# Per-head products with 64-row contraction: zero-padded 128-row operands replaced by row tiles in pairs of PSUM banks

## The reference, cut to what matters

```python
# attention scores of a head, 256 queries by the keys, 64 features summed
z = jnp.einsum('bhqd,bhkd->bhqk', qb, kb) * scale          # stick-breaking attention, 8 heads
# the same kind of product stands in the sparse attention (4 heads, two branches,
# and 15 compressed keys), in the retention (4 heads), and in the chunked RWKV
# recurrence, where for chunks c of 128 tokens and 4 heads
#   M_ab = b^T a, M_ak = k^T a, M_rb = b^T r, M_rk = k^T r   (128 x 128 each, 64 features summed)
```

## Time and profile before

| what | before |
|---|---|
| time, median of 3 (lowest, highest) | 2041.87 us (2037.39, 2044.82) |
| span of the profiled execution | 2041.5 us |
| PE busy, share of the span | 1951.0 us, 96% |
| PE weight loads | 1747.7 us, 86% |
| DVE busy | 1423.1 us, 70% |
| ACT busy | 1168.1 us, 57% |
| POOL busy | 76.5 us, 4% |
| mean granted TensorE clock | 0.990 |

### The profile page before, as it was taken

How to read it: one execution, slowest core, us unless ns; L and a number is a source line. 1 busy time by engine, 2 the same in 40 slices (tenths; PEclk the granted TensorE clock), 3 DMA queues, 4 the chain that set the end, 5 groups by cost and what they waited for, 6 DMA issues and landing times.

```text
span 2041.5 us, 29505 instructions
## 1 busy us (share of the span) xinstructions
PE 1951.0 (96%) x12546; PEld 1747.7 (86%) x12546; DVE 1423.1 (70%) x1424; ACT 1168.1 (57%) x1310; POOL 76.5 (4%) x94
## 2 busy tenths in 40 slices
PE   7999999999999999999999999999889999999997
PEld 6989998988998989999887999887778888888875
DVE  4586648546555677647745555757679999999996
ACT  4544344555444554334654444465388888888884
POOL 0000013000000000004000000000000000000000
PEclk9999999999999999999999999999999999999999
DMA  7333365534554443346544555433369999999993
GB/s 283 140 126 132 122 250 199 207 124 160 191 186 146 160 145 135 130 157 262 206 145 154 191 186 186 143 116 124 124 254 379 375 379 376 376 375 377 374 390 155
DMA packets 64520, 440.80 MB, mean 216 GB/s; under 512 B 7372, under 2 KB 7372, under 8 KB 14592
## 3 DMA queue, kind: packets, MB, share of 16 engines
q1 hardware_dynamic: 55296, 399.63, 52.4%
q0 software_dynamic: 8096, 35.30, 4.7%
q10 hardware_dynamic: 992, 3.93, 0.5%
HBM read 428.61 MB, written 10.23 MB: 215 GB/s over the span
## 4 chain that ended last, share of the span: by engine, by line
PE 64%; DVE 23%; ACT 8%; issue 2%; POOL 1%; DMA 1%; DVEq 0%; ACTq 0%; POOLq 0%
PE psum L188 63%; DVE ring_low L202 7%; ACT hl L198 4%; DVE arena L212 3%; DVE ht L202 3%; DVE rounded L202 2%; DVE hl L202 2%; DVE rounded L212 2%; DVE arena L202 2%; POOL arena L202 1%; ACT arena L198 1%; PE psum L192 1%; DVE resid L202 1%; ACT rounded L198 1%; ACT gn L198 1%
## 5 line engine op out<-in xcount | busy, mean ns | idle before, releaser
L202 DVE TENSOR_TENSOR hl<-ring,hl 128x2048 fp32r<-128x2048 f32 (+1 forms) x190 | 433.6, 2286 | 306.1 <-ACT hl L198 305.7
L188 PE MATMUL psum<-ht,hl 128*128 128x256 f32 x4992 | 621.6, 285 | 5.7 <-DVE ht L202 5.7
L188 PEld LDWEIGHTS psum<-ht,hl 128*128 128x128 f32 x4992 | 607.6, 192 | 14.3 <-DVE ht L202 6.6
L198 ACT ACTIVATE hl<-ring 128x2048 fp32r<-128x2048 f32 (+1 forms) x286 | 536.3, 1896 | 111.3 <-PE psum L188 105.2
L198 ACT ACTIVATE arena<-psum 128x512 f32<-128x512 f32 (+5 forms) x232 | 120.9, 521 | 405.8 <-PE psum L188 374.7
L188 PE MATMUL psum<-hl,ax 128*128 128x512 f32 x1320 | 346.3, 392 | 2.0 <-ACT gn L198 1.2
L188 PEld LDWEIGHTS psum<-hl,ax 128*128 128x128 f32 x1320 | 246.7, 188 | 53.9 <-ACT gn L198 1.7
L202 DVE TENSOR_TENSOR ring_low<-ring,hl 128x2048 fp32r<-128x2048 f32 x96 | 215.4, 2286 | 20.5 <-ACT hl L198 20.3
L188 PE MATMUL psum<-arena 128*128 128x128 f32 (+6 forms) x1520 | 186.6, 288 | 4.2 <-ACT arena L198 2.4
L188 PEld LDWEIGHTS psum<-arena 128*128 128x128 f32 (+2 forms) x1520 | 172.2, 178 | 15.0 <-ACT arena L198 3.6
L188 PE MATMUL psum<-rounded 128*128 128x512 f32 (+2 forms) x640 | 132.4, 335 | 5.9 <-DVE par L202 3.2
(11 more groups left out here) (123 smaller groups left out, 2030.6 us busy)
## 6 DMA issues: line engine op xcount, KB each, us to landing
ring<-W SPq DMA_DIRECT2D x284, 1024.0 KB, 5.2
arena<-W SPq DMA_DIRECT2D x48, 1024.0 KB, 8.1
ht_raw<-W SPq DMA_DIRECT2D x46, 1024.0 KB, 7.8
gate_d<-arena POOLq DMA_DIRECT2D x32, 256.0 KB, 3.9
arena<-gate_d POOLq DMA_DIRECT2D x8, 1024.0 KB, 8.2
gn<-GB POOLq DMA_DIRECT2D x10, 512.0 KB, 4.3
arena<-GB POOLq DMA_DIRECT2D x6, 512.0 KB, 5.3
ring<-W SPq DMA_DIRECT2D x4, 512.0 KB, 5.2
```

The costliest lines, as they stand in the source:

```text
L188: return Nothing() if self.e is None else self.e.matmul(o, a, b, start=start, stop=stop, skip_group_check=skip_group_check)
L198: return self.e.activation(o, a, f, bias=bias, scale=scale)
L202: return Nothing() if self.e is None else self.e.tensor_tensor(o, a, b, op)
```

## The change

Where a product sums over one head's 64 rows, both operands are now taken on those 64 partitions only, `es = slice(64 * e, 64 * e + 64)`. TensorE then works as two row tiles of 64 rows. The even head's products go to one bank, the odd head's to another, and the two heads alternate instruction by instruction. The zero-padded copies go: `L.qz` becomes `L.q2` (one ACT copy of 128 x 512), `L.rq` becomes `L.rq2` (one DVE addition), `aPz` and `rPz` are no longer made (the products read `aP` and `rP`), `b2.zq` is written in one piece for each pair of slabs; the memsets on DVE and POOL and POOL's two waits before them go too.

Banks: a new method `Banks.two` gives the pairs for the scores, for `sc` and for M, always two neighbouring banks (2n and 2n + 1), because DVE reads both in one instruction. Retention and second-block scores take two ordinary turns.

```diff
+    def two(self, *names):
+
+        turn = self.now["turn"]
+        first = next(b for b in turn if b ^ 1 in turn)
+        out = []
+        for b, name in zip((first & ~1, first | 1), names):
+            turn.remove(b)
+            turn.append(b)
+            out.append((b, self.now["had"].get(b)))
+            self.now["had"][b] = name
+        return out
@@ tensor
+            def pair(*name):
+
+                for e, (b, before) in enumerate(turn.two((*name, 0), (*name, 1))):
+                    if before in freed:
+                        of, n = freed[before]
+                        pe.wait_ge(of.sem, n)
+                    banks[(*name, e)] = b
+                return banks[(*name, 0)], banks[(*name, 1)]
@@ scores of the sparse attention: 2 pairs for each branch in place of 4 single banks
-                            for e in range(2):
-                                ins = mm(psum[:, b, 256 * e:256 * e + nk],
-                                         [(L.qz[:, 2 * hp + e, 128 * t:128 * t + 128], kT[:, 0:nk])])
-                            ins.then_inc(s_pe, P("s", br, t, hp, l))
+                        two = pair("s", br, t, l)
+                        for j in range(2):
+                            for e in range(2):
+                                es = rows_of(e)
+                                ins = mm(psum[:, two[e], 256 * j:256 * j + nk],
+                                         [(L.q2[es, j, 128 * t:128 * t + 128], kT[es, 0:nk])])
+                        ins.then_inc(s_pe, P("s", br, t, l))
@@ compressed keys: one pair in place of one bank
-                b = bank("sc", l)
+                two = pair("sc", l)
@@ retention
-                    mm(psum[:, b, 0:256], [(L.rk[:, h // 2, 0:128], L.rq[:, h, :])])
-                    mm(psum[:, b, 256:384], [(L.rk[:, h // 2, 128:256], L.rq[:, h, 128:256])]).then_inc(s_pe, P("att", h, l))
+                            ins = mm(psum[:, two[e], o], [(L.rk[es, j, c:c + 128], L.rq2[es, j, c:256])])
@@ RWKV: four pairs of banks in place of eight banks, two products of every head in a pair
-                for nm, c in (("ab", 0), ("ab", 1), ("ak", 0), ("rb", 0), ("rk", 0), ("ak", 1), ("rb", 1), ("rk", 1)):
-                    b = bank("M", nm, c, l)
-                        ins = mm(psum[:, b, 128 * h:128 * h + 128],
-                                 [(lt[:, h // 2, 128 * c:128 * c + 128], rt[:, h, 128 * c:128 * c + 128])])
-                    ins.then_inc(s_pe, P("M", nm, c, l))
+                for n, both in enumerate(M_PAIRS):
+                    two = pair("M", n, l)
+                                ins = mm(psum[:, two[e], o], [(lt[es, j, cs], rt[es, j, cs])])
+                    ins.then_inc(s_pe, P("M", n, l))
@@ second block: for each pair of heads
+                two = [bank("z", hg, e) for e in range(2)]
+                        ins = mm(psum[:, two[e], o], [(b2.k[es, hg, c:c + 128], b2.zq[es, hg, c:256])])
@@ scalar
-                ac.wait_ge(s_dve, V["qz0", l])
-                for h in range(4):
-                    e = 64 * (h % 2)
-                    copy(L.qz[e:e + 64, h, :], half(banks["q", l], h // 2)[e:e + 64, :], "qz", l)
+                copy(L.q2, half(banks["q", l]), "q2", l)
@@ vector
-                mset(flat(L.qz), 0.0, "qz0", l)
-                mset(flat(L.rq), 0.0)
-                            tt(L.rq[es, h, :], L.raw[es, h // 2, :], L.tmp4[es, h // 2, :], ADD)
+                        tt(L.rq2, rw, L.tmp4, ADD)
-                    copy(L.aPz[es, h, :], L.aP[es, h // 2, :])
-                    copy(L.rPz[es, h, :], L.rP[es, h // 2, :], "aPz", l)
-            mset(flat(b2.zq), 0.0)
@@ vector: scores, read across the pair; the compressed scores in two instructions, not one
-                            stt(Sp[:, hs, :], half(banks["s", br, t, hp, l])[:, :, 0:nk], 0.125, L.bm[:, hs, mo_:mo_ + nk],
+                            stt(Sp[:, hs, :], across(two)[:, :, 256 * hp:256 * hp + nk], 0.125, L.bm[:, hs, mo_:mo_ + nk],
@@ pool
-                gp.wait_ge(s_pe, P["ro", 1, l])
-                gp.wait_ge(s_dve, V["att", 3, l])
-                gp.memset(flat(L.aPz), 0.0).then_inc(s_pool, G("aPz"))
-                gp.memset(flat(L.rPz), 0.0).then_inc(s_pool, G("aPz0", l))
```

More of the change, by code:

```diff
@@ L337, in flat, with across, rows_of, by_row @@
             return ap.rearrange("p a b -> p (a b)")
+        def across(two):
+            return psum[:, two[0]:two[0] + 2, :]
+        def rows_of(e):
+            return slice(64 * e, 64 * e + 64)
+        def by_row(ap):
+            return ap.rearrange("p (j e) n -> p e j n", e=2)
         def again(ap, c):
@@ L810, in tensor @@
                 fill()
-                for h in range(4):
-                    b = bank("att", h, l)
+                for j in range(2):
+                    two = [bank("att", 2 * j + e, l) for e in range(2)]
                     pe.wait_ge(s_dve, V["rk", l])
-                    mm(psum[:, b, 0:256], [(L.rk[:, h // 2, 0:128], L.rq[:, h, :])])
-                    mm(psum[:, b, 256:384], [(L.rk[:, h // 2, 128:256], L.rq[:, h, 128:256])]).then_inc(s_pe, P("att", h, l))
+                    for c, o in ((0, slice(0, 256)), (128, slice(256, 384))):
+                        for e in range(2):
+                            es = rows_of(e)
+                            ins = mm(psum[:, two[e], o], [(L.rk[es, j, c:c + 128], L.rq2[es, j, c:256])])
+                    ins.then_inc(s_pe, P("att", j, l))
                 pe.wait_ge(s_dve, V["rkr", l])
@@ L2113, in scores @@
                         mo_ = 128 * (1 - t)
+                        two = tuple(banks["s", br, t, l, e] for e in range(2))
+                        ve.wait_ge(s_pe, P["s", br, t, l])
                         for hp in range(2):
                             hs = slice(2 * hp, 2 * hp + 2)
-                            ve.wait_ge(s_pe, P["s", br, t, hp, l])
                             ve.wait_ge(s_hank, 48 + 16 * l)
-                            stt(Sp[:, hs, :], half(banks["s", br, t, hp, l])[:, :, 0:nk], 0.125, L.bm[:, hs, mo_:mo_ + nk],
+                            stt(Sp[:, hs, :], across(two)[:, :, 256 * hp:256 * hp + nk], 0.125, L.bm[:, hs, mo_:mo_ + nk],
                                 MUL, ADD)
-                            gone("s", br, t, hp, l)
+                            if hp:
+                                for e in range(2):
+                                    gone("s", br, t, l, e)
                             red(f[:, hs, 0:1], Sp[:, hs, :], MAX)
@@ L2142, in vector @@
                 ve.wait_ge(s_pe, P["sc", l])
-                stt(Sv, psum[:, banks["sc", l], 0:256].rearrange("p (a n) -> p a n", n=32)[:, :, 0:15], 0.125, L.BC, MUL, ADD)
-                gone("sc", l)
+                two = tuple(banks["sc", l, e] for e in range(2))
+                for e in range(2):
+                    stt(by_row(Sv)[:, e], psum[:, two[e], 0:128].rearrange("p (a n) -> p a n", n=32)[:, :, 0:15], 0.125,
+                        by_row(L.BC)[:, e], MUL, ADD)
+                    gone("sc", l, e)
                 red(st[:, :, 0:1], Sv, MAX)
@@ L2252, in vector, with masked @@
                 lower(oT[1], L.rcen, "oT", 1, l)
-                def masked(nm, c):
-                    mk = C("s_lt_t" if nm[0] == "a" else "s_le_t").unsqueeze(1).broadcast_to([128, 4, 128])
-                    ve.wait_ge(s_pe, P["M", nm, c, l])
-                    tt(L.M[nm, c], heads4(banks["M", nm, c, l]), mk, MUL, "M", l)
-                    gone("M", nm, c, l)
+                def masked(n, i):
+                    nm, c = M_PAIRS[n][i]
+                    mk = C("s_lt_t" if nm[0] == "a" else "s_le_t").unsqueeze(1).unsqueeze(1).broadcast_to([128, 2, 2, 128])
+                    two = tuple(banks["M", n, l, e] for e in range(2))
+                    ve.wait_ge(s_pe, P["M", n, l])
+                    tt(by_row(L.M[nm, c]), across(two)[:, :, 256 * i:256 * i + 256].rearrange("p e (j n) -> p e j n", j=2),
+                       mk, MUL, "M", l)
+                    if i:
+                        for e in range(2):
+                            gone("M", n, l, e)
                 def level(i, c):
@@ L2264, in vector @@
                 for c in range(2):
-                    masked("ab", c)
+                    masked(0, c)
                     level(0, c)
-                for nm in ("ak", "rb", "rk"):
-                    masked(nm, 0)
+                for i in range(2):
+                    masked(1, i)
                 fill()
@@ L2276, in vector @@
                     level(1, c)
-                for nm in ("ak", "rb", "rk"):
-                    masked(nm, 1)
+                for n in (2, 3):
+                    for i in range(2):
+                        masked(n, i)
                 fill()
@@ L2506, in vector @@
                 rec(b2.rb, b2.rb)
[L2507 to L2509 removed]
+                stt(b2.zq[:, i:i + 2, :], b2.q[i // 2], b2.qg[:, 0:1], b2.rb, MUL, MUL, "zq", i // 2)
             unit()
```

53 lines of the change are left out of this document (25 added, 28 removed).

## The result

The changed kernel takes 2057.22 us (median of 5 runs, 2056.62 to 2060.02) against 2041.87 for the kernel before: ratio 1.0083, interval 1.0062 to 1.0104, so slower by less than 1%. On a later chip the same two gave 2057.54 and 2038.17, ratio 1.0091 (1.0057 to 1.0126): 19.4 us apart, and not 15.4. The forecast was 2052.7 with 2042 to 2061: right in sign and mechanism, 4.5 us short in size. Set against the 2041.9 of the kernel before its upper end stands for +19.1, which the later pair passes by a hair. Two kinds of terms were clearly mis-sized: the clock behind the new waits costs more than was said, and the gain at the start of layer 0 isn't there in every execution. The profiled execution has a span of 2058.2 us, 16.7 over before. Its own time is 2060.02, 1.8 us more than its span.

The account below looks back on a forecast made before the run. TensorE, busy for 96% of the span, was taken as the bound, with its waits deciding. The terms summed to +10.8 us, set on 2041.9 us: 2052.7 us, range 2042 to 2061.

Parts of the forecast that it names:

- 1 start of layer 0: Start of layer 0: the memset of L.qz that TensorE waits for goes, -0.9 us; layer 1 gains 0.
- 2 clock at the start: Clock behind the wait at layer 0's start: its fall may not come; ends 0 and -5.2, taken as -2.5 us.
- 3 scores and sc: First scores and sc: TensorE waits for newest banks; +5.8 us in layer 0, +4.4 in layer 1, sum +10.2.
- 4 clock in sc and the fill behind it: Clock behind the new idle stretches of 6.4 and 6.7 us: +1.5 each, +3.0 us; ends 0 and +3.8.
- 5 gates and retention: Gates and retention: memset of L.rq goes, four additions become one; -1.86 us in each layer, -3.7 in all.
- 6 M: M: waits for the bank ACT reads late, then runs in half the time; +0.45 us each, +0.9.
- 7 clock in and behind M: Clock behind M's new idle 3.7 us: +1.5 each, +3.0 us; ends 0 and +3.8.
- 8 second block: Second block: wait +0.2, scores 3 -0.25, sum 0.0 us; clock behind its longer wait +0.8 (0 to +1.7).
- A: The forecast itself: bank waits and the clock behind them make it slower; 2052.7 us, from 2047 to 2058; chance 0.60.
- B: Bank waits come, but the clock does not suffer and layer 0 starts at full clock; +1.3, 2043 us; chance 0.17.
- C: Head of the turn even at sc and M, so the pair is oldest and TensorE goes on; -17.8, 2024 us; chance 0.10.
- D: Row tiles of 64 rows with f32 data run one after the other; 2063.6 us; chance 0.13.

Follow-up runs that it names:

- e1_oldest: The changed kernel with one line altered: every pair of banks is the one whose younger bank is oldest; 2033.4 us, ratio 0.9983 to the kernel before.
- experiment 4: The kernel before with only DVE's memset of L.qz moved behind the next two units of weights, no row tiles; 2036.64 us, ratio 0.9996.
- experiment 3: The changed kernel with dummy products while TensorE waits before sc and the first M, the waits kept; 2046.61 us, ratio 1.0045 to the kernel before.
- experiment 1: Same run as e1_oldest: the changed kernel taking the pair whose younger bank is oldest, everywhere; 2033.4 us, ratio 0.9983 to the kernel before.
- e4_hold: Same run as experiment 3: the changed kernel with dummy products in the waits before sc and the first M; 2046.61 us, ratio 1.0045.
- e6_ret: The kernel before with the L.qz memset moved and, of the change, the retention part alone; 2032.45 us, ratio 0.9975 to the kernel before.
- e7_ret_m: e6_ret plus M as pairs of row tiles, in the pair whose younger bank is oldest; 2031.24 us, ratio 0.9976 to the kernel before.
- e5_memset_later: Same run as experiment 4: the kernel before with only the memset of L.qz moved behind two units of weights; 2036.64 us, ratio 0.9996.
- e2_sc_oldest: The changed kernel with the pair whose younger bank is oldest for sc alone; 2043.7 us, ratio 1.003 to the kernel before.

## Why the prediction was right, and where not

Terms by the account above, predicted and measured, both layers together where both have them:

```
step                                     predicted   measured
1 start of layer 0                         -0.9       -0.95
2 clock at the start                       -2.5       -4.88   (-5.83 + 0.95)
3 scores and sc                           +10.2       +9.0    (5.40 + 3.62)
4 clock in sc and the fill behind it       +3.0       +6.8    (3.46 + 3.33)
5 gates and retention                      -3.7       -4.7    (-2.34, -2.33)
  clock behind the retention's wait         0         +2.5    (1.23 + 1.24)
6 M                                        +0.9       +0.7    (0.39 + 0.35)
7 clock in and behind M                    +3.0       +5.4    (2.70 + 2.70)
8 second block                             +0.0       +0.05
  clock there                              +0.8       +1.4
untouched places                            0         +1.3    (2.35 + 0.27 - 1.36)
sum                                       +10.8      +16.7
```

How the lines split: in step 3 of layer 0 the difference goes from -5.83 to +0.40, 6.23, of which 0.83 are the clock inside `sc` (1.82 us, 0.99 to 1.0 with the clock held); in layer 1 from +7.36 to +11.81, less the same 0.83. In M the difference grows by 3.09, of which 6.47 - 3.77 = 2.70 are clock. The 2.35 at untouched places lie at two short stretches of low clock after M of layer 0 (0.72 over 347.2 to 352.2 us and over 474 to 480 us); the second profile of the changed kernel has them too.

**The count of the banks (3, 6) held.** The pair at `sc` and at M waits for the newest bank, in both layers, and the first scores of layer 0 for `cmp` (1.59 us). The predicted start of `sc`, 81.4 on the scale of before, was 75.42 + 5.83 = 81.25. In layer 1 it was 720.81 - 7.36 = 713.45 against 714.04: DVE's chain began when it had begun before (700.04 - 7.36 = 692.68 against 692.67), and not 0.3 us later, and ended 0.3 earlier; with `sc` at 0.99 and not 1.15 us that term came out 0.8 smaller. The scores take less time than with full height: 16 records of branch 2 in 1.51 us (61.48 to 62.99) where the earlier trace rows had 2.42, so 0.9 saved as said; M at full clock takes 3.77 us where 3.5 and a switch of 0.2 were predicted. Two row tiles of 64 rows with f32 data run side by side, as the earlier trace rows had let expect of smaller ones.

**The clock (2, 4, 7) is where the sum failed.** For 4 and 7 I carried over the loss behind idle 3.14 us from the earlier trace rows, 1.7 and 1.4 us, to idle 6.4 and to a stage of other shape. Behind `sc` the half clock lasted some 8 us and cost 3.4 us, more than twice the term and above its upper end (3.8 for both layers; measured 6.8). Behind M it was 2.7 a layer. The reason in the trace is that the clock was at 0.50 from the first record in both and stayed there for nearly 8 and nearly 6 us, where I had counted 4 us at about 0.6. Behind the retention scores, where I had put no clock term because the wait stays, the idle was as before (3.16 us), but the low clock lasted longer: 0.50 and then 0.72 over the next 4 us, where the first profile of before has 0.57 and then 1.00. That is another 1.2 us in each layer. It can't be laid to the change: the second profile of the kernel before has 0.50 and 0.72 at this place of layer 0, and `e1_oldest`, with the same halved products, 1.00. The Trainium skill (TensorE: Matmul & The Clock Gate, Part 1) says that TensorE's default is throttled and that activity releases the throttle; the rows agree with that, and the dummy products, which keep it active, removed the loss at all three places.

**Step 2 was sized from one execution.** The middle of two ends was taken, and in the profiled pair the whole 4.9 us came; but with another execution of the kernel before there is nothing to gain, as experiment 4 shows. So in the median over executions the term seems to be near zero (two profiles of the kernel before don't tell how often the fall comes). The later chip, where the change stands 19.4 us above before and not 15.4, agrees. That the sum came as near as it did is in part luck: in the profiled pair the terms that were too small come to 10.6 us (the clock, and the untouched places) and those that were too large, or gained more than was said, to 4.8. The text had said that the runs may hold executions of either kind; a term that hangs on this should have been taken at 0, with the whole loss as its other end.

**Step 5** was right in both parts: from the products with v to the small row tiles the difference falls from +2.43 to +1.79 in layer 0 (-0.64, -0.76 predicted), and behind the retention scores by 1.10, as predicted. One thing came on top: 0.60 us, a wait for ACT before the products with v (idle 0.53 us in the kernel before) that the later TensorE no longer meets. That is the other face of the waits: what is late itself finds less to wait for.

**The range of A.** With all of its ends at once the lower one is 2043.2 (the whole gain at the start and no loss of clock, which is B) and not 2047; the upper one, 2057.7, is as it was written. It changes nothing in the forecast.

**The rivals.** B (no loss of clock) gave 2043: experiment 3 is its world made by hand, 2046.6. C (parity even) gave 2024, 17.8 us under the kernel before: experiment 1 is its world, and it reached 2033.4, 4.2 under the kernel before on its chip. I had let TensorE flow through the probabilities' transposes, where the chain of DVE and ACT ends later (2.7 us a layer), and M saved 1.9 us a layer and not 3.1; the start of layer 0 (3.4 us of the sum) brought nothing in the median. The remainder was not traced. D fell by the 59 ns a record. The Trainium skill (TensorEngine Tiling (Array Packing), PSUM Bottleneck) says that tiling speeds up TensorE but not the evacuation of PSUM. The wait of 1.15 us inside M of experiment 1, for ACT's copies of `tm`, is of that kind; the wait before the transposes of the probabilities is for DVE's softmax and is not.

## What to carry to other kernels

When a change needs banks in pairs, write out which stage wrote each of the two last and when it is read: the younger of the two sets the start, and one line that picks another pair was worth 20 to 24 us here. Price a new idle stretch of TensorE with the clock behind it (here 3.1 to 3.5 us of loss behind 6.4 us of idle, 1.6 to 2.7 behind 3.5), as large as the saving hoped for; dummy products in the wait gave it back. Read such a loss from more than one profile: behind the same idle 3.16 us it was anything from nothing to 2.8 us. Halving products that stand before a wait for DVE or ACT gains nothing; by the predicted terms the gain of this change was in the small edits on DVE (the retention: 4.2 us), and a second execution of the kernel before would have shown that one of its stalls comes and goes.

## What the runs showed of the hardware

- Row tiles of 64 rows with f32 data: M's records of 128 columns at 59 ns in turn, 80 ns in groups of eight, 110 ns as full-height products, all at full clock. In turn they start in pairs 7 ns apart, a pair every 106 ns (`e4_hold`).
- The clock behind one and the same idle differs from execution to execution. Behind the retention scores TensorE is idle for 3.13 to 3.17 us in nearly every kernel. From the end of this wait to the end of the next fill it takes 6.80 us in both layers of `e1_oldest` (clock 1.00), 8.3 to 8.4 in both layers of the first profile of before, of `e6_ret` and of `e7_ret_m` (0.57 and 0.66 in the first profile of before), and 9.5 to 9.6 in both layers of the changed kernel, in both its profiles, and in layer 0 of the second profile of before (0.50, then 0.72). Idle 2.29 us at the same place of `e5_memset_later` was followed by 1.00.
- M behind idle 3.53 us took 6.42 to 6.47 us in both profiles of the changed kernel, but 5.40 in layer 0 of `e2_sc_oldest`; at full clock it is 3.77. The fill behind `sc` and idle 6.4 us took 8.1 to 8.5 us in all six stages that have this wait, 5.85 at full clock.
- In the first profile of before, the products ran for 2.1 us at full clock behind the idle 0.93 us ahead of 43.86, and only then, from 46.0 us on, at 0.50. Whether that wait had to do with the fall stays open.
- Executions of one kernel differ by some 2 us in their first 45 us: the products of 140 columns start at 43.86 and 45.53 us in the two profiles of before, at 42.91 and 40.54 in those of the changed kernel. In the second profile of before TensorE waits 2.48 us there for a transfer from `scratch`, in the first it doesn't. They differ again by where short falls of the clock lie.
